# First attention: the scores of a unit one slot sooner on TensorE, directly behind the transposes of the probabilities of unit u - 2

## What is computed

```python
s = jnp.einsum('bcqhgd,bcshd->bchgqs', qc, kb) * (A_HEAD_DIM ** -0.5)
s = jnp.where(valid[None, :, None, None], s + bias, -1e30)
m = jnp.maximum(jnp.max(s, axis=-1, keepdims=True), sink)
p = jnp.exp(s - m)
denom = jnp.sum(p, axis=-1, keepdims=True) + jnp.exp(sink - m)
o = jnp.einsum('bchgqs,bcshd->bcqhgd', p / denom, vb)
```

## Time and profile before

| | us |
|---|---|
| median of three runs | 548.93 (548.21 to 549.0) |
| the profiled execution | 548.88 |
| its span in the trace | 547.1 |
| PE busy | 535.0 (98%) |
| DVE busy | 420.3 (77%) |
| ACT busy | 353.9 (65%) |
| stretch of the attention, slots 3 to 18 | about 62 to 126 |

### The profile page before, as it was taken

One profiled execution on the slowest core, in us unless ns is written; L12 is line 12 of the kernel. 1 busy time (PEld: TensorE's weight loads), 2 busy tenths in 40 slices (PEclk: granted clock), 3 DMA queues, 4 the chain that ended last, 5 costly groups with the idle time before them and its releaser, 6 DMA issues.

```text
span 547.1 us, 7888 instructions
## 1 busy us (share of the span) xinstructions
PE 535.0 (98%) x2685; PEld 438.7 (80%) x2686; DVE 420.3 (77%) x572; ACT 353.9 (65%) x474; POOL 96.3 (18%) x117
## 2 busy tenths in 40 slices
PE   7999999999999999999999999999999999999994
PEld 5988777777877888898878888888888888888883
DVE  5563599564865853388999889898989898898986
ACT  5563654770226263356877887888787887888745
POOL 3260000000000000034330224122221222110520
PEclk8999999999999999999999999999999999999998
DMA  8999122323020236658999999999999999999894
GB/s 318 374 288 401 44 75 78 77 79 76 2 78 0 78 115 228 236 211 277 399 380 377 373 380 395 375 375 365 381 363 364 373 385 382 371 393 396 264 211 177
DMA packets 63739, 143.78 MB, mean 263 GB/s; under 512 B 3811, under 2 KB 13339, under 8 KB 63584
## 3 DMA queue, kind: packets, MB, share of 16 engines
q1 hardware_dynamic: 56528, 120.24, 61.7%
q0 software_dynamic: 7040, 22.66, 13.5%
q10 hardware_dynamic: 144, 0.52, 0.3%
HBM read 132.51 MB, written 14.30 MB: 268 GB/s over the span
## 4 chain that ended last, share of the span: by engine, by line
PE 88%; DVE 6%; ACT 2%; issue 2%; DMA 1%; ACTq 0%; POOL 0%; DVEq 0%; POOLq 0%
PE ps L1577 25%; PE ps L1579 24%; PE ps L1578 24%; PE ps L1584 7%; DVE lo_ring L1366 2%; PE ps L1728 2%; PE ps L1714 2%; PE ps L1690 1%; PE ps L1660 1%; PE ps L1755 1%; DMA arena<-norm_g 1%; PE ps L1845 1%; DVE act_lo L1064 0%; ACT arena L762 0%; ACT hi_ring L744 0%
## 5 line engine op out<-in xcount | busy, mean ns | idle before, releaser
L1366 DVE TENSOR_TENSOR lo_ring<-arena,hi_ring 128x2048 fp32r<-128x2048 f32 x94 | 213.8, 2288 | 24.7 <-ACT hi_ring L925 24.7
L1577 PE MATMUL ps<-hi_ring,act_hi 128*128 128x512 f32 x576 | 230.0, 399 | 0.3 <-DVE act_lo L1217 0.2
L1579 PE MATMUL ps<-hi_ring,act_lo 128*128 128x512 f32 x576 | 224.9, 390 | 0.0
L1578 PE MATMUL ps<-lo_ring,act_hi 128*128 128x512 f32 x576 | 224.3, 389 | 0.0
L925 ACT ACTIVATE hi_ring<-arena 128x2048 fp32r<-128x2048 f32 x94 | 180.2, 1917 | 26.7 <-PE ps L1579 26.7
L1579 PEld LDWEIGHTS ps<-hi_ring,act_lo 128*128 128x128 f32 x576 | 108.1, 188 | 23.3
L1577 PEld LDWEIGHTS ps<-hi_ring,act_hi 128*128 128x128 f32 x576 | 108.2, 188 | 22.9 <-issue 1.6
L1578 PEld LDWEIGHTS ps<-lo_ring,act_hi 128*128 128x128 f32 x576 | 108.4, 188 | 20.8
L1054 DVE SCALAR_TENSOR_TENSOR lo_ring<-arena,over,hi_ring 128x512 fp32r<-128x512 f32 x40 | 29.3, 748 | 29.4 <-ACT hi_ring L744 29.2
L1064 DVE TENSOR_TENSOR act_lo<-ps,act_hi 128x512 fp32r<-128x512 f32 x56 | 36.8, 683 | 6.4 <-ACT act_hi L777 5.9
L1584 PE MATMUL ps<-keep,arena 128*128 128x128 f32 x260 | 35.2, 275 | 1.2 <-DVE arena L1074 0.7
(11 more groups left out here) (242 smaller groups left out, 518.4 us busy)
## 6 DMA issues: line engine op xcount, KB each, us to landing
arena<-w_gate SPq DMA_DIRECT2D x32, 1024.0 KB, 16.7
arena<-w_up SPq DMA_DIRECT2D x32, 1024.0 KB, 17.6
arena<-w_down SPq DMA_DIRECT2D x32, 1024.0 KB, 15.2
arena<-w_in SPq DMA_DIRECT2D x16, 512.0 KB, 7.3
y_dram<-arena POOLq DMA_DIRECT2D x8, 512.0 KB, 11.2
res<-y_dram POOLq DMA_DIRECT2D x8, 512.0 KB, 9.7
arena<-w_in SPq DMA_DIRECT2D x2, 1024.0 KB, 10.7
arena<-w_out SPq DMA_DIRECT2D x4, 512.0 KB, 6.4
```

The costliest lines, as they stand in the source:

```text
L1366: nc.vector.tensor_tensor(lo(N1 + n12), raw(n12), hi(N1 + n12).bitcast(F32), ALU.subtract).then_inc(lo_done, 1)
L1577: nc.tensor.matmul(dst, a_hi, b_hi, start=start, stop=False)
L1578: nc.tensor.matmul(dst, a_hi, b_lo, start=False, stop=False)
L1579: return nc.tensor.matmul(dst, a_lo, b_hi, start=False, stop=stop)
```

## The change

TensorE gets a table of its own for the scores. Unit 0 keeps slot 0. Unit 1 moves from slot 2 to slot 1, behind the transposes of the values' input (`turn_v`). Unit u from 2 on moves from slot 2u to slot 2u - 1, behind `turn_prob(u - 2)`. VectorE, ScalarE, GpSimd and the queues keep their order instruction for instruction, and every wait is kept, that of the scores for `logit_ready` among them.

```diff
 TURN_V_SLOT = 1
 SCORE_SLOTS = tuple(range(0, 16, 2))
+PE_SCORE_SLOTS = (0,) + tuple(range(1, 15, 2))
 DENOM_SLOTS = tuple(range(2, 18, 2))
...
                 if k in TURN_SLOTS:
                     turn_prob(TURN_SLOTS.index(k))
-                if k in SCORE_SLOTS:
-                    scores(SCORE_SLOTS.index(k))
+                if k in PE_SCORE_SLOTS:
+                    scores(PE_SCORE_SLOTS.index(k))
```

## The result

| | before, us | after, us |
|---|---|---|
| median of five runs | 548.30 (548.13 to 549.0) | 551.74 (551.38 to 552.75) |
| the profiled execution | 548.88 | 552.75 |
| its span | 547.1 | 550.9 |

The changed kernel is slower: 1.0059 times the time of before, 95% interval 1.0042 to 1.0076, 3.44 us between the medians. That is about 0.2 us above the forecast of +3.27 us.

The account below looks back on a forecast made before the run. TensorE was taken to bound the kernel. Waits of 1.56 + 1.29 + 0.69, less 0.42 saved, plus 0.15 unit 1 could not keep, gave 3.27 us; on 548.93 that made 552.2, range 550.4 to 554.0.

Parts of the forecast that it names:

- What bounds, and that nothing is gained: Attention: TensorE bounds, busy 63.68 of 64.00 us; DVE does not wait for scores, so earlier scores start nothing sooner.
- DVE's waits for the high halves: Low half of a weight piece waits for ACT's high half: 24.4 us in eight places, to stay as long.
- The walk through the units: Attention units 1 to 7: when TensorE reaches each moved score against when DVE ends the logits before; sum 3.27 us.
- The lengths of the waits: TensorE before the scores of units 2, 5 and 7: waits of 1.56, 1.29 and 0.69 us.
- The release: Time from DVE's end of logits to TensorE's waiting scores: 0.05 us, upper bound 0.32, at three waits up to 0.8 more.
- The start of scores behind transposes: TensorE, scores directly behind full-height transposes: in no row; 0.15 us taken from product into scores, seen only behind the last wait.
- The third term: ACT at unit 4's step: copy at 71.16, so unit 2's exponentials start at 71.75 instead of 70.75, 1.0 us late.
- That nothing later gives it back: After the attention: TensorE runs without a gap and weight transfers start later by as much, so the 3.27 us stays.
- The clock: Rival, chance 0.08: new idle time lowers TensorE's granted clock, 1.7 us for one fall, 3.4 for two: 553.9 to 555.6.
- The partly hidden case: Rival, chance 0.10: most of the delay is hidden by earlier logits or later slack, +0.3 to +2.2 us, 549.2 to 551.1.
- the faster one: Rival: scores gate DVE's logits after all, 0.74 us less, 548.2; chance 0.06 for no effect or faster.
- The three more switches: TensorE, where scores stood between values and transposes: three more tiling-mode switches, 3 x 0.15 = 0.45 us at most.

Follow-up runs that it names:

- unit 3 alone: Only unit 3's scores moved one slot sooner, against the kernel before: 549.42 against 548.26 us, ratio 1.0018.
- the three units that wait: Only the scores of units 2, 5 and 7 moved one slot sooner, against the kernel before: 552.40 against 548.67 us, ratio 1.0065.
- the kernel with the early release: Full change, but scores wait only until VectorE has read their two banks, against the kernel before: 549.45 against 548.67 us, ratio 1.0012.
- unit 5 alone: Only unit 5's scores moved one slot sooner, against the kernel before: 550.64 against 548.67 us, ratio 1.0035.

## Why the prediction was right

**What bounds, and that nothing is gained.** Right: no wait of DVE for scores turned up, and DVE's and ACT's busy times are the same (420.3 and 353.8 against 420.3 and 353.9). One sign of the prediction did not come: DVE's waits for the high halves did not stay as long as before. They went from 24.4 us in eight places to 26.3 in ten, which costs nothing by itself, since TensorE waits for none of them:

```profile
DVE lo_ring L1055 <- ACT hi_ring L745: 26.3, 10, 5.2
```

**The walk through the units.** All times of the new trace lie 0.11 later than those of the old from slot 1 on (52.59 against 52.48). With that taken off, the ends of the logits that set the waits came to within a few hundredths of the walk: unit 1 at 64.01 (64.01 foretold), unit 4 at 88.77 (88.81), unit 6 at 107.02 (106.97). Which units wait (2, 5, 7) and which find their wait over (3, 4, 6) was right, and unit 3 alone showed that this hangs on the delay that TensorE already has.

**The lengths of the waits.** From the end of the transposes to the scores it was 1.69, 1.03 and 0.65 (64.27 - 62.58, 89.03 - 88.00, 107.28 - 106.63, with transposes of 0.38 and 0.79 as in the walk) against 1.56, 1.29 and 0.69 foretold: the first longer, the others shorter. The idle times in brackets, 1.42, 0.78 and 0.40, are smaller by another 0.25 to 0.27, since they count from the end of the last matmul's row, which runs past the start of what follows.

Three terms of the walk were mis-sized. The release was put at 0.05, from a row of ACT, and took 0.15 on TensorE, three times; each would make TensorE 0.10 later, 0.3 in the sum. The start of scores behind transposes, 0.17 each, was given bounds and left out of the walk; it makes TensorE arrive later (at the transposes of unit 3 by 87.10 - 85.43 = 1.67 instead of 1.35), and so shortens the waits at units 5 and 7 by as much as it adds. That it costs nothing there was said and held: the three units that wait gave +3.48, all seven +3.46. The third term had the other sign: the walk let the exponentials of unit 2 follow ACT's copy after its whole length, 0.59, but they start 0.48 behind its start. The timeline of ACT:

```profile
71.36 0.59 ACT L814 COPY arena<-ps 128x512 f32<-128x512 f32 x1 [4.22 <-PE ps L1585]
71.84 0.46 ACT L807 ACTIVATE arena<-arena,stat 128x192 f32<-128x192 f32 x1
```

With the 0.11 taken off they start at 71.73, where the walk had 71.75, though the release at unit 2 had made TensorE 0.10 later. Two small errors cancelled there, which is luck. So of the 0.3 only half arrived: the scores of unit 7 start at 107.17 against 107.02, and 3.27 + 0.15 = 3.42 of the 3.46 in the stretch is accounted for.

**That nothing later gives it back.** Right: +3.46 in the stretch, +3.44 in the medians, and the loop of the experts is TensorE without a gap before and after.

**The rivals.** The clock stayed at 1.00 in the window that holds all three waits. The partly hidden case and the faster one did not come. The rule of the Trainium skill (TensorEngine Tiling (Array Packing), Key Properties), that changing the tiling mode drains TensorE, agrees with the 0.17; it would have made the change slightly slower even with no wait, and the kernel with the early release is slower, by 0.90 in the stretch with 0.2 of a wait in it. The three more switches that the prediction counted are those at units 3, 5 and 7, where 0.67 of it lies; the prediction had put them at 0.45 at most.

What the runs leave open: whether the 0.17 and the 0.67 are this drain or another cost of the change from transposes to scores. No run takes the two apart. No version beat the kernel before. Its stretch has 0.32 us of idle TensorE in all, so there is little that an order of this kind could win.

## What to carry to other kernels

Before making an instruction earlier on the busiest engine, look at whether its reader waits for it, and at what it waits for itself: here the reader was never waiting, and the tile product between transposes and scores was the cover of a block of VectorE's work. Where two steps on one engine hang on two consecutive steps of another, the distance between them must be at least the length of the second; put directly behind each other, the difference is idle time, and since the end of the wait is set by the other engine, prices do not add up unit by unit: unit 3 waited 1.13 us alone and not at all once unit 2 had waited. A wait should be for the instruction that frees the resource and not for the last of its block: that alone took away 2.7 of the 3.4 us.

## What the runs showed of the hardware

A release from VectorE reached a waiting matmul of TensorE after 0.15 us at three scores and 0.14 at the transposes of unit 7, where ScalarE started 0.04 us behind the instruction that released the first of them (end of L1136 at 64.12, this row of ACT):

```profile
64.16 0.40 ACT L807 ACTIVATE arena<-arena,norm_tmp 128x128 f32<-128x128 f32 x1 [0.69 <-DVE norm_tmp L1136]
```

Scores on 64 rows of the array start 0.17 us later behind transposes than a product of full height does (0.96 against 0.79). Idle times of 1.42 us here and 1.46 with unit 5 alone, amid otherwise full work, did not lower TensorE's granted clock: it is 1.00 from 62 to 129 us here, and from 86 to 94 us there.
